# Six modulation chunks moved inside a trunk layer, and constant matrix products ahead of two waits of the router

## The chip, the cores and the metric

One core of a Trainium2 chip runs the whole program. The metric is device time in microseconds, launch to end, of that core. The program is written engine by engine: TensorE (PE in the profile), VectorE (DVE), ScalarE (ACT), GpSimd (POOL) and SyncE (SP) each have their own instruction list, and semaphores join them. All arithmetic is in float32. Weights are read from HBM while the program runs.

## What is computed

Two layers (`DEPTH = 2`) are run over 384 tokens, 128 of a context and 256 of a latent grid, with 1024 features. Cut to what the change touches:

```python
for l in range(DEPTH):
    sh1, sc1, g1, sh2, sc2, g2 = modulation(cond, P['w_mod'][l], P['b_mod'][l])
    h = rmsnorm(x, P['norm1_w'][l]) * (1 + sc1) + sh1
    u_att, u_rw, u_ssd = split_cols(h @ P['w_in'][l], [ATT_COLS, RW_COLS, SSD_COLS])
    # attention, RWKV-7 recurrence and SSD (its output goes through rmsnorm(y * silu(z)))
    x = x + g1 * (o @ P['w_out'][l])
    h = rmsnorm(x, P['norm2_w'][l]) * (1 + sc2) + sh2
    x = x + g2 * moe(h, ...)      # 16 experts, 4 groups, best group, best two experts in it
```

`modulation` is `silu(cond) @ w_mod + b_mod` with a 1024 x 6144 matrix for each layer and two rows of `cond` only: little arithmetic, but 24 MB of weights for a layer. It depends on nothing else in the layer, so it can be done anywhere before its result is read.

## The kernel before

**Layout.** Features lie on partitions and the 385 columns (`W`; one is a gap) are tokens. Weights come in items of 128 x 2048 float32 (1 MB) through homes in on-chip memory: five slots of a ring, and, in the experts' stage, three places in `sb_u`, four in `sb_arena`, one in `sb_sq` and one in `sb_hT`. From attention to the fourth column block of the output projection only ring slots 0 and 1 are open to dense items (`KEPT = 2`), since the mixers use the rest as scratch.

**Modulation chunks.** Each layer's modulation is cut into 12 chunks. A chunk (`mod` in `fill`, L1032) is two weight items and 64 recorded products `sb_ring,sb_scond` of 128 columns, whose stationary tile is 32 wide; ScalarE then copies the result to `mod_rows`. One place later a product with the identity (`modT`, L1006) turns it, and VectorE adds the bias (`sb_mod`); for chunks 3 and 9 VectorE also computes a scale (`scale1`, `scale2`). The table `MOD_AT` (L58) says how many chunks lie at each of the named places, and each engine calls `fill(l, place)` at that place in its list.

**Order of one layer on TensorE.** `mean_square` 1; `in_projection`; `attention`; `RW_ORDER` (`rw_order`, L150), a hand-written interleaving of the batched inverses, six recurrence steps (each: `values`, `carry`, `solve`, `state`, `output`; the last has no `state`) and SSD's small steps; `mixer_ends` (L1379: RWKV's group norm `gnm` and `gnv`, SSD's outputs `ys` for three tiles, then SSD's mean square `yms`); `out_projection` (eight blocks `out`); `mean_square` 2; `moe` (router logits `lg`, 24 transposes `hm`, nine small products `pos` that count tokens ahead of each token, the gather `xp` by products with a 0/1 matrix, then the experts: 12 blocks, up to 11 more for full experts, and four held ones).

**What sets the order around the change.** On VectorE, `ssd_states` (new SSD states) stands ahead of the last `carry`, whose result the last `solve` needs. SSD's gate on VectorE (`ssd_gate`) makes the squares that `yms` needs; ScalarE turns `yms` into a root (`inverse_root`: Ln, a table load, Exp), `ssd_norm` writes `sb_o` and releases `mix_ready`, on which the output projection waits. Behind `hm`, TensorE waits for `assigned_ready`, set by a chain of some 36 small VectorE instructions (`routing`); `pos` feeds a second such chain, which ends in `picks_ready`, on which the gather waits. The chunks at place `rows` stand between `pos` and the gather.

**The load order.** `weight_stream` lists the items in the order of their use, `homes_of` (L403) gives each a home by least recent use, and SP issues the loads in one list; each waits until the item that was in its home has been read (`home_free`). PSUM's eight banks are given out in the order of the same plan (`open_bank`).

Of the kernel before, what the change touches and what calls it, by code (L numbers as in the profile page):

```python
# [16 lines left out]
TILES = 3  # L17
# [36 lines left out]


MOD_CHUNKS = 12
MOD_PLACES = ["start", "norm1", "sc0", "sc2", "pv1", "pv2", "rw", "rw2", "ssd", "norm2", "rows", "held", "tail"]
MOD_AT = {(0, "start"): 2, (0, "norm1"): 2, (0, "sc0"): 1, (0, "sc2"): 1, (0, "pv1"): 1, (0, "pv2"): 1,  # L58
          (0, "rw"): 1, (0, "rw2"): 1, (0, "ssd"): 1, (0, "norm2"): 1, (0, "rows"): 2, (0, "tail"): 1,
          (1, "norm1"): 1, (1, "sc0"): 1, (1, "sc2"): 1, (1, "pv1"): 1, (1, "pv2"): 1, (1, "rw"): 1,  # L60
          (1, "ssd"): 1, (1, "norm2"): 1, (1, "rows"): 1}

# [85 lines left out]
def rw_order():  # L150

    out = []
    behind = {0: [], 2: [("factors", 0), ("factors", 1)] + recurrence(0) + recurrence(1),
              4: [("factors", 2), ("factors", 3)] + recurrence(2) + recurrence(3)}
    for first in (0, 2, 4):
        extra = behind[first]
        for n, step in enumerate(RW_STEPS):
            out += [(step, first), (step, first + 1)] + SSD_BESIDE.get((first, step), [])
            k = -(-len(extra) // (len(RW_STEPS) - n))
            out += extra[:k]  # L160
            extra = extra[k:]
    out += [("ssd_ends", 0), ("factors", 4), ("factors", 5)] + recurrence(4)
    return out + [("ssd_states", 0)] + recurrence(5)


RW_ORDER = rw_order()
# [41 lines left out]
def psum_plan():  # L208
# [4 lines left out]
    def g(consumer, *key):  # L213
        plan.append((key, consumer))
# [5 lines left out]
    for l in range(DEPTH):  # L220
# [100 lines left out]
        for t in range(1, TILES):  # L321
            for grp in range(2):
                g("v", "ys", l, t, grp)
        g("a", "yms", l)
        for n in range(KT):
            g("v", "out", l, n)
# [76 lines left out]
def homes_of(stream, plan):  # L403
# [48 lines left out]
    def free_at(n):  # L452

        if before[n] is not None:
            return order_of[stream[before[n]][1]]
        l = stream[n][0][1]
        return order_of["ms", l, 2] if HOMES[home[n]][0] == "sq" else order_of["hm", l, TILES - 1, 1]

    for l in range(DEPTH):
        first = [n for n in loads if stream[n][0][:2] == ("expert", l) and  # L460
                 (HOMES[home[n]][0] in ("sq", "hT") if before[n] is None else stream[before[n]][0][0] == "fixed")]
        at = sorted(loads.index(n) for n in first)
        assert at == list(range(at[0], at[0] + len(at)))
        loads[at[0]:at[0] + len(at)] = sorted(first, key=lambda n: (free_at(n), n))
        more = [n for n in loads if stream[n][0][:2] == ("expert", l) and stream[n][0][2] >= EXPERTS]
        loads = [n for n in loads if n not in more]
        at = loads.index(next(n for n in loads if stream[n][0] == ("expert", l, STORED, 0)))
        loads[at:at] = more
# [4 lines left out]
def program(nc, a):  # L473
# [6 lines left out]
    with ctx:  # L480
# [506 lines left out]
        def _(pe):  # L987
# [17 lines left out]
            def tr(out, in_, n=P):  # L1005
                return nc.tensor.transpose(out, in_, C("ident")[0:n, 0:n])  # L1006

            def mean_square(l, which):

                bank = open_bank(pe, "ms", l, which)  # L1010
                if which == 1 and l:
                    for t, (lo, hi) in enumerate(TILE_COLUMNS):
                        pe.wait_ge(xsq_ready, KT * 2 * l + t + 1)
                        for k in range(KT):
                            last = mm(bank[:, lo:hi], C("ones"), sq[:, k, lo:hi], k == 0, k == KT - 1)
                else:
                    for k in range(KT):
                        pe.wait_ge(xsq_ready, KT * (2 * l + which - 1) + k + 1)
                        last = mm(bank[:, 0:W], C("ones"), sq[:, k, :], k == 0, k == KT - 1)
                last.then_inc(psum_filled, 1)  # L1020
                if which == 1 and l:
                    fill(l, "start")
                fill(l, f"norm{which}")
# [355 lines left out]
            def mixer_ends(l):  # L1379
# [10 lines left out]
                fill(l, "ssd")  # L1390
                ssd_output(l, 1)
                ssd_output(l, 2)
                bank = open_bank(pe, "yms", l)
                pe.wait_ge(gated_sq_ready, l + 1)
                for i in range(2):
# [34 lines left out]
            def moe(l):  # L1430
# [17 lines left out]
                            tr(bank[:, 0:32 * TILES], logits, 32 * TILES).then_inc(psum_filled, 1)  # L1448

                bank = open_bank(pe, "pos", l)  # L1450
                pe.wait_ge(assigned_ready, l + 1)
                for t in range(TILES):
                    for i in range(t):
# [7 lines left out]
                def gathered():  # L1461

                    for k in range(KT // 2):
                        bank = open_bank(pe, "xp", l, k)
                        if k == 0:
                            pe.wait_ge(picks_ready, l + 1)
                            taken(pe, "hm", l, TILES - 1, 1)
                        for i in range(2):
# [144 lines left out]
        def _(act):  # L1613
# [295 lines left out]
            for l in range(DEPTH):  # L1909
# [10 lines left out]
                logarithms(both, 64, "eps_gn", [("gnv", l, i) for i in range(2)])  # L1920
                f(both, both, ACT.Exp, scale=-0.5).then_inc(gn_root_ready, 1)
                fill(l, "ssd")
                inverse_root(ssd_root, 256, "eps", "yms", l)
                squares(l, 2)
                moe(l)
# [3 lines left out]
        def _(dve):  # L1929
# [676 lines left out]
            for l in range(DEPTH):  # L2606
# [48 lines left out]
                ssd_output(l, 1)  # L2655
                ssd_output(l, 2)
                ssd_gate(l)
                rwkv_output(l)
                ssd_norm(l)
                for n in range(KT):  # L2660
# [174 lines left out]
```

## Time and profile before

| | |
|---|---|
| median of 3 runs | 1154.85 us (1154.1 to 1165.44) |
| the profiled execution: its time | 1162.96 us |
| its span in the trace | 1161.2 us |
| mean granted clock of TensorE, as a share of full speed | 0.932 |
| busy share of the span: PE, PE weight loads, DVE, ACT, POOL | 86%, 59%, 41%, 25%, 7% |
| data moved by DMA | 238.58 MB, 205 GB/s on average |

The profile holds one execution. Its page gives, for 40 equal slices of the span (29 us each), the busy share of each engine in tenths, the clock that TensorE was granted and the load of the 16 DMA engines. The timeline lists instructions in order of time, neighbours of one kind merged ("x16" are 16 records; a float32 product leaves two records), with the idle time of the engine ahead of them in brackets and what ended it. TensorE's records are split into products (PE) and weight loads (PEld). [...]

### The profile page before, as it was taken

Reading aid. Unit: us, or ns where it says so; the run is one execution under the profiler, and the core shown is the slowest. Engines: PE = TensorE matmul, PEld = TensorE weight load, DVE = VectorE, ACT = ScalarE, POOL = GpSimd, SP = SyncE. Lnnn points to the kernel's source line nnn. Section 1 sums busy time; section 2 is a strip of 40 time slices with the busy share of each in tenths; the row PEclk is TensorE's granted clock in tenths of the full one; section 3 lists DMA queues with packets and bytes.
Section 4 is the critical chain, followed back from the end, with each engine's and each line's share of the span. In section 5 each row is a group of like instructions: output and inputs, shape, how many; then the busy total and the mean of one; then the engine's idle time right before and its main releaser. Section 6 shows DMA issues by size and latency. Waiting matters only on the chain. (4 is left out here: it accounts for less than half of the span.)

```text
span 1161.2 us, 24556 instructions
## 1 busy us (share of the span) xinstructions
PE 1000.5 (86%) x10657; PEld 685.0 (59%) x10657; DVE 481.0 (41%) x1331; ACT 294.9 (25%) x610; POOL 78.8 (7%) x127
## 2 busy tenths in 40 slices
PE   3999999988879789867989998999987968996686
PEld 2555657788545575534755565778864556653365
DVE  1261567487431433111636166647843142311125
ACT  2331335432210511110143133543221141111000
POOL 0000000000000032221000000000000002221110
PEclk7999999999879799998999999899998978999789
DMA  9769433212156489999742221222025647999992
GB/s 385 267 157 302 108 109 146 80 72 81 60 225 263 181 323 333 361 378 376 290 176 73 73 77 73 110 111 76 8 76 238 244 173 268 385 352 375 359 410 63
DMA packets 41908, 238.58 MB, mean 205 GB/s; under 512 B 5121, under 2 KB 8193, under 8 KB 18369
## 3 DMA queue, kind: packets, MB, share of 16 engines
q1 hardware_dynamic: 29904, 196.27, 44.9%
q0 software_dynamic: 11888, 40.64, 11.3%
q8 instruction: 89, 1.46, 0.5%
q14 instruction: 27, 0.21, 0.1%
HBM read 210.15 MB, written 26.74 MB: 204 GB/s over the span
## 5 line engine op out<-in xcount | busy, mean ns | idle before, releaser
L1003 PE MATMUL bank<-sb_hT,sb_ring 128*128 128x385 f32 (+1 forms) x640 | 214.6, 493 | 4.4 <-ACT sb_hT L1623 4.4
L1003 PEld LDWEIGHTS bank<-sb_hT,sb_ring 128*128 128x128 f32 (+1 forms) x640 | 119.9, 189 | 94.0 <-issue 13.4
L1003 PE MATMUL bank<-sb_ring,sb_arena 128*64 128x256 f32 (+4 forms) x768 | 118.4, 411 | 24.8 <-DMA sb_ring<-weights 13.0
L1623 ACT ACTIVATE sb_arena<-bank 128x128 f32<-128x128 f32 (+5 forms) x108 | 44.4, 426 | 307.3 <-PE bank L1003 242.6
L1003 PEld LDWEIGHTS bank<-sb_ring,sb_arena 128*64 128x64 f32 (+2 forms) x768 | 70.6, 155 | 61.0 <-issue 31.3
L1623 ACT ACTIVATE sb_u<-bank 128x256 f32<-128x256 f32 (+3 forms) x104 | 47.7, 475 | 217.7 <-PE bank L1003 208.0
L1003 PE MATMUL bank<-sb_arena 64*64 64x64 f32 (+5 forms) x984 | 91.0, 329 | 6.1 <-DVE sb_arena L2508 1.9
L1003 PE MATMUL bank<-sb_o,sb_ring 128*128 128x385 f32 x256 | 88.6, 509 | 8.0 <-issue 8.0
L1940 DVE TENSOR_TENSOR sb_arena<-sb_arena,bank 128x128 f32<-128x128 f32 x67 | 17.8, 286 | 159.0 <-ACT sb_arena L1623 152.0
L1003 PEld LDWEIGHTS bank<-sb_o,sb_ring 128*128 128x128 f32 x256 | 50.8, 199 | 46.8 <-issue 15.0
L1943 DVE SCALAR_TENSOR_TENSOR sb_xT<-bank,sb_mod,sb_xT 128x128 f32<-128x128 f32 (+1 forms) x128 | 37.8, 360 | 92.1 <-PE bank L1003 92.0
L1003 PEld LDWEIGHTS bank<-sb_arena 64*64 64x64 f32 (+2 forms) x984 | 56.7, 146 | 31.9 <-issue 19.6
L1003 PE MATMUL bank<-sb_u,sb_arena 64*64 64x64 f32 (+2 forms) x760 | 65.1, 318 | 7.0 <-DMA sb_u<-weights 2.4
L1003 PE MATMUL bank<-sb_ring,sb_scond 128*32 128x128 f32 x1536 | 54.1, 299 | 12.5 <-DMA sb_ring<-weights 12.3
L1003 PE MATMUL bank<-sb_u 64*64 64x64 f32 x1592 | 55.7, 224 | 5.8 <-DVE sb_u L1940 4.4
L1003 PEld LDWEIGHTS bank<-sb_u 64*64 64x64 f32 x1592 | 51.3, 139 | 12.1 <-DVE sb_u L1940 6.3
L1003 PE MATMUL bank<-sb_u,sb_o 64*128 64x128 f32 (+2 forms) x576 | 51.6, 292 | 6.6 <-issue 6.1
L1003 PEld LDWEIGHTS bank<-sb_ring,sb_scond 128*32 128x32 f32 x1536 | 45.8, 120 | 19.0 <-issue 9.4
L1003 PE MATMUL bank<-sb_sq,sb_consts 128*128 128x385 f32 (+2 forms) x148 | 45.2, 456 | 11.4 <-DVE sb_sq L1940 6.0
L2624 DVE COPY sb_u<-bank 128x385 f32<-128x385 f32 x20 | 11.2, 558 | 102.1 <-PE bank L1003 102.1
L1003 PEld LDWEIGHTS bank<-sb_u,sb_o 64*128 64x128 f32 (+2 forms) x576 | 44.7, 183 | 14.0 <-issue 9.1
L1003 PEld LDWEIGHTS bank<-sb_u,sb_arena 64*64 64x64 f32 (+1 forms) x760 | 38.6, 137 | 24.2 <-issue 14.8
(209 smaller groups left out, 1238.1 us busy)
## 6 DMA issues: line engine op xcount, KB each, us to landing
sb_ring<-weights SPq DMA_DIRECT2D x116, 1024.0 KB, 8.4
sb_arena<-weights SPq DMA_DIRECT2D x29, 1024.0 KB, 18.4
sb_u<-weights SPq DMA_DIRECT2D x20, 1024.0 KB, 11.7
sb_sq<-weights SPq DMA_DIRECT2D x8, 1024.0 KB, 17.0
sb_hT<-weights SPq DMA_DIRECT2D x8, 1024.0 KB, 19.3
x_slots<-sb_o POOLq DMA_DIRECT2D x1, 6912.0 KB, 39.7
y_slots<-sb_arena POOLq DMA_DIRECT2D x54, 128.0 KB, 7.1
sb_sq<-x_slots POOLq DMA_DIRECT2D x18, 256.0 KB, 7.8
```

Of the source, the lines that this page charges most:

```text
L1003: return nc.tensor.matmul(out, lhsT, rhs, start=start, stop=stop, skip_group_check=True)
L1623: return nc.scalar.activation(out, in_, func, **kw)
L1940: return v.tensor_tensor(out, x, y, op)
L1943: return v.scalar_tensor_tensor(out, x, s, y, op0, op1)
L2624: v.tensor_copy(u[:, tile, 1:W + 1], bank[:, 0:W]).then_inc(read("u", l, c), 1)
```

## The change

The table of chunks gets two new places. `rw3` lies in the last recurrence step, behind `carry`, and `gate` lies behind SSD's last output, ahead of `yms`. Place `rows` is emptied in both layers (two chunks in layer 0, one in layer 1), and so is `norm2` in layer 1. Since chunks are dealt out in order, layer 0 now does its chunk 10 at `rw3`, its chunk 11 at `ssd`, and layer 1's chunks 0 and 1 at `gate` and `norm2`; layer 1 does its chunks 9, 10 and 11 at `rw3`, `ssd` and `gate`. The number of chunks is the same. In the planner, an expert's item may now have a ring slot as its first home (it then waits for `mix_ready`), and such items are sorted in with the others.

`keep_warm` is new: products of two constants, 128 x 128 by 385 columns, into a bank that the next real product overwrites. Five stand ahead of the wait for `assigned_ready`, seven ahead of the wait for `picks_ready`.

```diff
-MOD_PLACES = ["start", "norm1", "sc0", "sc2", "pv1", "pv2", "rw", "rw2", "ssd", "norm2", "rows", "held", "tail"]
+MOD_PLACES = ["start", "norm1", "sc0", "sc2", "pv1", "pv2", "rw", "rw2", "rw3", "ssd", "gate", "norm2", "rows", "held", "tail"]
 MOD_AT = {(0, "start"): 2, (0, "norm1"): 2, (0, "sc0"): 1, (0, "sc2"): 1, (0, "pv1"): 1, (0, "pv2"): 1,
-          (0, "rw"): 1, (0, "rw2"): 1, (0, "ssd"): 1, (0, "norm2"): 1, (0, "rows"): 2, (0, "tail"): 1,
+          (0, "rw"): 1, (0, "rw2"): 1, (0, "rw3"): 1, (0, "ssd"): 1, (0, "gate"): 1, (0, "norm2"): 1, (0, "tail"): 1,
           (1, "norm1"): 1, (1, "sc0"): 1, (1, "sc2"): 1, (1, "pv1"): 1, (1, "pv2"): 1, (1, "rw"): 1,
-          (1, "ssd"): 1, (1, "norm2"): 1, (1, "rows"): 1}
+          (1, "rw3"): 1, (1, "ssd"): 1, (1, "gate"): 1}
...
-    return out + [("ssd_states", 0)] + recurrence(5)
+    out += [("ssd_states", 0)]
+    for step in recurrence(5):
+        out.append(step)
+        if step[0] == "carry":
+            out.append(("fill", "rw3"))
+    return out
...
+        fill(l, "gate")
         g("a", "yms", l)
...
-        return order_of["ms", l, 2] if HOMES[home[n]][0] == "sq" else order_of["hm", l, TILES - 1, 1]
+        return order_of[{"ring": ("yms", l), "sq": ("ms", l, 2), "hT": ("hm", l, TILES - 1, 1)}[HOMES[home[n]][0]]]
...
-                 (HOMES[home[n]][0] in ("sq", "hT") if before[n] is None else stream[before[n]][0][0] == "fixed")]
+                 (HOMES[home[n]][0] in ("sq", "hT", "ring") if before[n] is None else stream[before[n]][0][0] == "fixed")]
...
+            def keep_warm(bank, n):
+
+                for _ in range(n):
+                    mm(bank[:, 0:W], C("head"), C("restart"))
...
                 ssd_output(l, 2)
+                fill(l, "gate")
                 bank = open_bank(pe, "yms", l)
                 pe.wait_ge(gated_sq_ready, l + 1)
...
                 bank = open_bank(pe, "pos", l)
+                keep_warm(bank, 5)
                 pe.wait_ge(assigned_ready, l + 1)
...
                         if k == 0:
+                            keep_warm(bank, 7)
                             pe.wait_ge(picks_ready, l + 1)
...
                 fill(l, "ssd")
+                fill(l, "gate")
                 inverse_root(ssd_root, 256, "eps", "yms", l)
...
                 ssd_gate(l)
+                fill(l, "gate")
                 rwkv_output(l)
```

The last two hunks are in ScalarE's list and in VectorE's, the three before them in TensorE's.

## Rows read from the trace of the kernel before

**Rows 1.** The page's 40 slices: granted TensorE clock, DMA load.

```profile
PEclk7999999999879799998999999899998978999789
DMA  9769433212156489999742221222025647999992
```

**Rows 2.** Windows of the experts' stages: stretch, length, busy of engines, clock, DMA share, GB/s.

```profile
410.00:430.00 20.00, 17.25 (x151) 14.39 (x141) 5.05 (x18) 4.48 (x11) 6.60 (x6) 1.00 0.96 370
...
510.00:530.00 20.00, 13.07 (x87) 6.84 (x87) 2.23 (x6) 2.45 (x5) 4.16 (x8) 0.83 1.02 363
...
1060.00:1080.00 20.00, 9.32 (x72) 4.96 (x68) 2.09 (x5) 1.99 (x5) 4.04 (x8) 0.80 1.02 347
```

**Rows 3.** Timeline, last recurrence step, both layers: start, length, instruction, idle before.

```profile
299.20 0.40 PE L1003 MATMUL bank<-sb_arena,sb_hT 64*64 64x64 f32 x12
...
301.90 0.68 PE L1003 MATMUL bank<-sb_tmp,sb_u 64*64 64x64 f32 x16 [2.29 <-DVE sb_tmp L1940]
...
853.36 1.07 PE L1003 MATMUL bank<-sb_tmp,sb_u 64*64 64x64 f32 x16 [2.29 <-DVE sb_tmp L1940]
```

**Rows 4.** Timeline, group norm (gnm) and the chunk at ssd, both layers.

```profile
305.32 2.90 PE L1003 MATMUL bank<-sb_arena,sb_consts 128*128 128x385 f32 x4 [0.80 <-DVE sb_arena L2327]
...
311.49 0.14 PEld L1006 LDWEIGHTS bank<-sb_consts,sb_mod_rows 128*128 128x128 f32 x1
...
312.01 1.95 PE L1003 MATMUL bank<-sb_ring,sb_scond 128*32 128x128 f32 x64
...
857.79 1.53 PE L1003 MATMUL bank<-sb_arena,sb_consts 128*128 128x385 f32 x4 [0.81 <-DVE sb_arena L2327]
...
862.52 1.95 PE L1003 MATMUL bank<-sb_ring,sb_scond 128*32 128x128 f32 x64
```

**Rows 5.** Timeline, SSD's mean square (yms) and what follows; its twin in layer 1.

```profile
325.88 2.90 PE L1003 MATMUL bank<-sb_sq,sb_consts 128*128 128x385 f32 x4 [2.65 <-DVE sb_sq L1940]
...
331.27 1.41 DVE L1943 SCALAR_TENSOR_TENSOR sb_o<-sb_arena,sb_small 128x128 f32<-128x128 f32 x4 [1.70 <-ACT sb_arena L1623]
...
332.78 12.56 PE L1003 MATMUL bank<-sb_o,sb_ring 128*128 128x385 f32 x30 [4.00 <-issue]
...
876.40 1.98 PE L1003 MATMUL bank<-sb_sq,sb_consts 128*128 128x385 f32 x4 [2.65 <-DVE sb_sq L1940]
```

**Rows 6.** Timeline, norm2 of layer 1, router and gather, and two full-clock references.

```profile
934.62 0.17 DVE L1943 SCALAR_TENSOR_TENSOR sb_scale<-sb_mod,sb_consts 128x16 f32<-128x16 f32 x1
...
401.73 3.99 PE L1003 MATMUL bank<-sb_arena,sb_consts 128*128 128x16 f32 x18 [4.85 <-DVE sb_arena L1940]
...
405.75 0.21 DVE L2457 COPY sb_arena<-bank 128x48 f32<-128x48 f32 x1 [4.18 <-PE bank L1003]
...
413.67 10.60 PE L1003 MATMUL bank<-sb_u,sb_o 128*128 128x256 f32 x48 [1.95 <-issue]
...
963.63 13.50 PE L1003 MATMUL bank<-sb_u,sb_o 128*128 128x256 f32 x48 [4.18 <-issue]
...
926.52 5.35 PE L1003 MATMUL bank<-sb_sq,sb_consts 128*128 128x385 f32 x16
...
85.06 0.82 PE L1006 MATMUL bank<-sb_consts,sb_arena 128*128 128x128 f32 x6
```

**Rows 7.** Windows of layer 0 between two changes of the clock, columns as in Rows 2.

```profile
303.90:310.60 6.70, 5.90 (x35) 3.73 (x32) 3.69 (x10) 0.40 (x1) 0.00 (x0) 0.50 0.00 0
...
392.70:396.00 3.30, 3.30 (x17) 3.30 (x16) 0.66 (x5) 2.84 (x5) 0.00 (x0) 0.50 0.23 97
396.10:399.40 3.30, 0.78 (x7) 0.54 (x5) 2.82 (x17) 1.59 (x4) 0.00 (x0) 1.00 0.44 117
...
401.80:405.70 3.90, 3.90 (x19) 3.90 (x19) 0.00 (x0) 0.00 (x0) 0.00 (x0) 0.50 0.00 0
```

**Rows 8.** DMA issues: KB each, median us to landing; at 313.9 us, and the page's.

```profile
sb_ring<-weights SPq DMA_DIRECT2D x1, 1024.0 KB, 4.8
...
sb_u<-weights SPq DMA_DIRECT2D x20, 1024.0 KB, 11.7
```

## The prediction

> **What bounds the kernel now.** I read the page's 40 slices first, for what kind of time each stage is made of [rows 1]. The clock row tells that TensorE is not held at full speed everywhere: slices of 7 and 8 tenths stand in the middle of both layers, around the end of the recurrence and the router. The DMA row tells the stages apart: it stands at 9 in the experts' stages and at 1 or 2 in the mixers. Then windows of the experts' stages [rows 2]: the transfers are saturated there (0.96 to 1.02), and TensorE is busy for 17.25 of 20 us at their start, but only for 13.07 and 9.32 us later. So this stage is bound by the transfers, and what precedes it by TensorE and by chains through VectorE and ScalarE. The change touches only the second kind. I therefore went to the timeline and looked, at each of the four places, for the idle time of TensorE and for the clock that it has behind it [rows 3 to 7].
>
> **Can the experts' stage swallow what is saved ahead of it?** Its transfers go on from slot to slot: a home is loaded again when its item has been read. Nine homes outside the ring and five in it are full of early experts' items before the first expert is computed, in both versions, and the first reload waits for the first expert's products. So stage and transfers start together, and a start that is t earlier ends t earlier. I let every saving pass.
>
> **The last recurrence step (rw3).** TensorE ends `carry` at 299.20 + 0.40 = 299.60 us and starts `solve` at 301.90, 2.29 us later, since VectorE does SSD's states first; layer 1 is alike [rows 3]. A turn and a chunk take 312.01 + 1.95 - 311.49 = 2.47 us at full clock [rows 4], the chunk alone 1.95. In layer 0 both go in (chunk 9 still has to be turned): 0.17 us late. In layer 1 there is no turn: 0. VectorE's bias (0.17 us, with chunk 9 also a scale of 0.17) and ScalarE's copy fall where both wait for `solve`. If the items were late or the clock low, the cover would be gone: the chunk would cost up to its own 1.95 us. The gain is the clock behind it. In layer 0 the idle stretch is followed by one at 0.50, from 303.9 to 310.6, and the group norm's products take 2.90 us [rows 4, 7]; in layer 1 they take 1.53. From gnm to the chunk at ssd it is 312.01 - 305.32 = 6.69 us in layer 0, less 311.49's turn ahead of the chunk (0.52), and 862.52 - 857.79 = 4.73 us in layer 1: 1.44 us to gain. Layer 1 pays earlier: from `solve` to gnm it takes 857.79 - 853.36 = 4.43 us against 305.32 - 301.90 = 3.42: 1.01 us to gain. But chunk 9's turn now stands ahead of layer 1's chunk at ssd, where TensorE has no gap: -0.5 (the 0.52 of layer 0). Sum: layer 0 +1.27, layer 1 +0.5.
>
> **Ahead of yms (gate).** TensorE idles 2.65 us in both layers [rows 5]; turn and chunk take 2.47: no cost. yms itself takes 2.90 us in layer 0 and 1.98 in layer 1; at full clock 1.53, as its twin gnm of the same shape [rows 4, 5]: 1.38 and 0.45 us. Behind yms stand Ln, a table load, Exp and VectorE's last step at 331.27, for which VectorE had waited 1.70 us. With the new bias ahead of it (0.17) it has 1.53 us left, so the 1.38 passes. Queued behind the two turns and copies is nothing else that is late. The chunk costs something elsewhere: it fills both open slots, so the first two items of the output projection can only be asked for when it has been read, at about 325.7 instead of 314.0. One item of 1 MB, asked for with idle queues, lands in 4.8 us [rows 8]: 330.5. It is wanted at 332.78 - 1.38 + 0.1 = 331.4 or so: 0.9 us to spare. The output projection's own cold start stays: the 4.00 us gap ahead of it is as long as before [rows 5].
>
> **norm2 of layer 1.** Without its chunk, the scale of chunk 9 (934.62, 0.17 us) leaves the head of VectorE's list [rows 6]: +0.2 us. The logits are paced by ScalarE, so the longer idle stretch of TensorE ahead of them costs nothing.
>
> **Five constant products and pos.** The idle time ahead of pos is 4.85 us, and pos takes 3.99 us for 18 records, at a clock of 0.50 [rows 6, 7]. A product of 385 columns takes 5.35 / 8 = 0.67 us at full clock [rows 6] and 2.90 / 2 = 1.45 at half [rows 5]. Five take 3.3 us: hidden. The clock at the end of the transposes is 1.00, and it fell during the idle stretch [rows 7]; if the five hold it, pos takes something between half of 3.99, 2.0, and 18 times 0.82 / 6, 2.5 us [rows 6]. I take 2.2: +1.8 us in each layer, all of it on the path, since VectorE waits 4.18 us for pos. Bounds: no gain if the clock falls again before pos, and 2.0.
>
> **Seven constant products, and the gather without chunks.** From pos to the gather it is VectorE's chain, 413.67 - 405.75 = 7.9 us. The chunks taken out were hidden by it (1.95 us of idle time behind them in layer 0, 4.18 in layer 1), so their removal alone gives nothing. Seven products take 4.7 us: hidden, with 2.8 us of idle time in layer 0 (behind one turn) and 3.2 in layer 1. The gather took 10.60 us with a gap of 1.95 ahead of it, and 13.50 with one of 4.18 [rows 6]. New gaps lie between: a gap of 2.65 us lost the clock ahead of yms in layer 0 (2.90 us) and half kept it in layer 1 (1.98) [rows 5]. I take the mean, 12.05, for each layer: -1.45 and +1.45, together 0; bounds 2 x 10.60 and 2 x 13.50, that is +2.9 and -2.9.
>
> [...] In the last slice before the idle stretch TensorE did nothing but transposes, at 0.50, and behind it the clock was 1.00 [rows 7]. [...]
>
> **The sum.** Layer 0: 1.27 + 1.38 + 1.8 - 1.45 = 3.0. Layer 1: 0.5 + 0.45 + 0.2 + 1.8 + 1.45 = 4.4. Together 7.4 us. The profiled execution took 1162.96 us, so it would take 1155.6; it is 8.1 us above the median of the runs, for reasons that one trace can't show. Taken off the median, 1154.85, the sum gives 1147.5 us.
>
> **Rivals.**
> - *The constants run at half clock.* Five then take 7.25 us against the 4.85 of the gap: pos starts 2.4 us late and gains at most 2.0. The 1.8 us turn into -0.6 in both layers, 4.8 us less: 1152.3. For it: pos itself, busy throughout, did not raise the clock (401.8 to 405.7 at 0.50 [rows 7]), and seven products at half clock take 10.2 us, more than the chain's 7.9. Against it: the 1.00 at 396.1. [...]
> - *The clock also holds to the gather.* Both gathers take 10.6 us, 2.9 more: 1144.6.
> - *The change doesn't do what it says.* The clock falls in the same places, only elsewhere in each: covers cost their 0.17 + 0.5 and give 0.2, so 1155.3. For it: group norm in layer 1 stood at full clock though it had no chunk [rows 4], so idle time alone doesn't decide.
> - *The head start of the transfers.* Four items in layer 0 and two in layer 1 are no longer loaded at the router. At 370 GB/s [rows 2] an item of 1.05 MB is 2.8 us: if the experts' stage were bound by its own total, layer 0 would gain up to 11 us, 1136.5. Against it: the homes are full anyway.
> - *Slower: the output projection waits for its first item.* Behind gate's chunk it lands in 4.8 us only if the queues are idle. The items of `sb_u`, asked for in bursts, landed in 11.7 [rows 8]: it would be 11.7 - 4.8 - 0.9 = 6.0 us late in each layer, 12 us: 1159.5. From a landing of 4.8 + 0.9 + 3.7 = 9.4 us on this mechanism alone makes the kernel slower. Against it: no transfer but these runs there.
>
> **Chances.** Forecast 0.47; clock holds to the gather 0.17; constants at half clock 0.13; no effect 0.10; head start 0.06; first item late 0.07. The range 1141 to 1156 us takes in the bounds of the gathers (2.9 us) and of pos, and the second, third and fourth case; it leaves out the head start and most of the late item. About one per cent (11.5 us) is what a measurement of this kernel can tell from no change. Faster by more needs the head start or the upper bounds together: 0.2. Slower by more needs a late item with an even longer landing, or a stall that I don't see: 0.05. The rest, 0.75, is within 1%.
>
> **What would show each step.** In the profile after: chunks in the two gaps, with `solve` less than 0.3 us later behind `carry`; gnm at about 1.5 us and a clock of 1.00 behind it in both layers; yms at 1.5 us; the first block of the output projection not waiting for a DMA; pos at 2.0 to 2.5 us; seven products that end ahead of the gather; the gathers between 10.6 and 13.5 us. The forecast is wrong if pos stays at 4 us, if the wait ahead of the output projection grows beyond 4 us, or if the experts' stage, from the first expert to the layer's end, changes its length by more than 2 us: then the saving was eaten or multiplied there.

## The result, and the profile after

The changed kernel took 1142.74 us (median of 4 runs, 1138.7 to 1143.35), the kernel before 1154.47 us in 4 runs beside it. The ratio of changed to before is 0.9863, with a 95% interval of 0.9818 to 0.9908: faster by 1.4%. Ratios, here and below, are taken over the fast runs alone, those at most 1.5% above the fastest run of their kernel on that chip, and so are not the quotients of the medians given beside them (1142.74 / 1154.47 is 0.990). The forecast was 1147.5 us, 0.6% faster. The time lies inside the range, but the gain is 1.4% by the ratio, which is 16 us, and 11.7 us by these medians, where 7.4 were forecast, and "faster by over 1%" had been given 0.2. Counted chunk by chunk, seven have a new place, four of those done in layer 0 and three of those done in layer 1, not the six of the title.

The profiled execution took 1142.84 us (span 1141.0), 20 us less than that of before. The page's clock and DMA rows, to be read against [rows 1]:

```profile
PEclk9999998999999889998999999999999979999889
DMA  9769532422169449999842221232027736999992
```

Of the five 7s of the clock row one is left, far into layer 1. (The first of the five stood at the very start, where nothing was changed.) The DMA row looks much as before; what it hides comes below.

The timeline of TensorE in the profile after, at the places of the change: the last recurrence step and the group norm in layer 0, then in layer 1 (to be read against [rows 3, 4]):

```profile
305.60 0.40 PE L1009 MATMUL bank<-sb_arena,sb_hT 64*64 64x64 f32 x12
305.94 0.33 PE L1012 MATMUL bank<-sb_consts,sb_mod_rows 128*128 128x128 f32 x1
306.19 1.96 PE L1009 MATMUL bank<-sb_ring,sb_scond 128*32 128x128 f32 x64
308.30 0.69 PE L1009 MATMUL bank<-sb_tmp,sb_u 64*64 64x64 f32 x16
...
311.70 1.53 PE L1009 MATMUL bank<-sb_arena,sb_consts 128*128 128x385 f32 x4 [1.00 <-DVE sb_arena L2342]
...
842.65 0.68 PE L1009 MATMUL bank<-sb_tmp,sb_u 64*64 64x64 f32 x16 [0.41 <-ACT sb_mod_rows L1637]
...
845.99 1.53 PE L1009 MATMUL bank<-sb_arena,sb_consts 128*128 128x385 f32 x4 [0.93 <-DVE sb_arena L2342]
```

Turn and chunk fill the gap. In layer 0 `solve` follows the chunk without a gap, in layer 1, where no turn stands, 0.41 us behind it. Next, the chunk at gate, yms and the output projection in both layers (against [rows 5]), and constants, pos and gather (against [rows 6]):

```profile
327.96 1.95 PE L1009 MATMUL bank<-sb_ring,sb_scond 128*32 128x128 f32 x64
330.43 1.53 PE L1009 MATMUL bank<-sb_sq,sb_consts 128*128 128x385 f32 x4 [0.51 <-DVE sb_mod L1955]
335.95 1.62 PE L1009 MATMUL bank<-sb_o,sb_ring 128*128 128x385 f32 x2 [4.00 <-DVE sb_o L1958]
...
864.71 1.53 PE L1009 MATMUL bank<-sb_sq,sb_consts 128*128 128x385 f32 x4 [0.51 <-DVE sb_mod L1955]
870.25 5.17 PE L1009 MATMUL bank<-sb_o,sb_ring 128*128 128x385 f32 x10 [4.00 <-DVE sb_o L1958]
...
398.39 3.40 PE L1009 MATMUL bank<-sb_consts 128*128 128x385 f32 x10
403.84 3.87 PE L1009 MATMUL bank<-sb_arena,sb_consts 128*128 128x16 f32 x18 [2.05 <-DVE sb_arena L1955]
407.80 6.22 PE L1009 MATMUL bank<-sb_consts 128*128 128x385 f32 x14
415.62 10.63 PE L1009 MATMUL bank<-sb_u,sb_o 128*128 128x256 f32 x48 [1.60 <-DVE sb_u L1955]
...
938.22 2.49 PE L1009 MATMUL bank<-sb_arena,sb_consts 128*128 128x16 f32 x18 [1.31 <-DVE sb_arena L1955]
940.55 6.15 PE L1009 MATMUL bank<-sb_consts 128*128 128x385 f32 x14
948.65 10.63 PE L1009 MATMUL bank<-sb_u,sb_o 128*128 128x256 f32 x48 [1.95 <-DVE sb_u L1955]
```

The output projection waits for `sb_o` and for no transfer, 4.00 us as before. pos is 3.87 us in layer 0 and 2.49 in layer 1. Both gathers take 10.63 us.

Where do the 20 us between the two profiled executions lie? The table gives stretches from the start of one step on TensorE to the start of the next (in the last row to the end of the last product), in us, out of the timelines of five kernels: before, the changed one in two executions, and two of the experiments below.

| layer, stretch | before | changed | changed again | chunks only | constants only |
|---|---|---|---|---|---|
| 0, start to gnm | 305.32 | 311.70 | 309.11 | 306.41 | 308.12 |
| 0, gnm to yms | 20.56 | 18.73 | 18.72 | 18.73 | 18.72 |
| 0, yms to output projection | 6.90 | 5.52 | 5.52 | 5.52 | 5.65 |
| 0, output projection to pos | 68.95 | 67.89 | 67.95 | 69.10 | 69.17 |
| 0, pos to gather | 11.94 | 11.78 | 11.65 | 11.94 | 13.85 |
| 0, gather to the tail's chunk | 162.96 | 155.87 | 155.07 | 156.32 | 159.02 |
| 1, tail's chunk to gnm | 281.16 | 274.50 | 275.26 | 279.96 | 273.54 |
| 1, gnm to yms | 18.61 | 18.72 | 18.72 | 18.72 | 20.59 |
| 1, yms to output projection | 5.98 | 5.54 | 5.53 | 5.53 | 6.91 |
| 1, output projection to pos | 69.26 | 67.97 | 68.81 | 68.00 | 69.32 |
| 1, pos to gather | 11.99 | 10.43 | 10.92 | 11.97 | 12.00 |
| 1, gather to the last product | 189.36 | 185.00 | 182.96 | 187.40 | 186.10 |

Two things stand out that the forecast did not have: layer 0's stretch behind the gather is 7 us shorter, and the two long stretches in which next to nothing was changed (start to gnm, tail's chunk to gnm) differ by 6 to 8 us between executions, in either direction.

### The profile page after: what moved, and what is told of

Same layout as the page of the kernel before. It is cut to its first block and busy times, and to the rows that moved or that the text cites. A ratio compares the mean times of both kernels' runs of the same rounds, so it can differ in the third digit from the quotient of the medians.

```text
span 1141.0 us, 24651 instructions
## 1 busy us (share of the span) xinstructions
PE 999.4 (88%) x10705; PEld 682.7 (60%) x10705; DVE 480.8 (42%) x1331; ACT 295.7 (26%) x610; POOL 79.1 (7%) x127
## 3 DMA queue, kind: packets, MB, share of 16 engines
q0 software_dynamic: 11888, 40.64, 11.7%
## 5 line engine op out<-in xcount | busy, mean ns | idle before, releaser
L1009 PE MATMUL bank<-sb_ring,sb_arena 128*64 128x256 f32 (+4 forms) x768 | 113.8, 398 | 34.4 <-PEq L1590 12.4
L1009 PE MATMUL bank<-sb_arena 64*64 64x64 f32 (+5 forms) x984 | 88.5, 323 | 5.0 <-DVE sb_arena L2523 1.9
L1009 PE MATMUL bank<-sb_ring,sb_scond 128*32 128x128 f32 x1536 | 50.9, 286 | 12.5 <-DMA sb_ring<-weights 12.4
L1009 PEld LDWEIGHTS bank<-sb_ring,sb_scond 128*32 128x32 f32 x1536 | 42.9, 115 | 18.0 <-issue 8.4
L1009 PE MATMUL bank<-sb_u,sb_o 64*128 64x128 f32 (+2 forms) x576 | 49.1, 287 | 4.6 <-DVE sb_u L1955 3.6
```

Source lines behind the costliest of these rows:

```text
L1009: return nc.tensor.matmul(out, lhsT, rhs, start=start, stop=stop, skip_group_check=True)
```

## Experiments

Each kernel ran beside the kernel before on the same chip, in five rounds. The kernel before had medians, over all its runs, of 1162.57 us (29 runs, 1148.57 to 1167.76), 1157.06 (16 runs) and 1162.52 (11 runs) on the three chips: the first for sections 1 and 2, the second for the changed kernel again, the loads held in layer 0, more constants and the tail's chunk at norm2, the third for the rest.

### 1. The chunks alone, and the constants alone

The change without its constants:

```diff
-                keep_warm(bank, 5)
-                            keep_warm(bank, 7)
```

> The changed kernel without its twelve constant products in a layer: only the chunks stand at their new places. Three theories of the 11.7 us that the change brought (1154.5 to 1142.7). (Sum as forecast) The chunks bring 1.27 + 1.38 us in layer 0 and 0.5 + 0.45 + 0.2 in layer 1, 3.8 together: about 1150.7; layer 0 from the gather to the tail's chunk as long as before, 163 us. (Head start of the transfers) Emptying the place rows frees the queues at the start of the experts' stage: layer 0 from gather to tail is about 156 us as after the change, 7 us shorter, and the kernel takes 1144 to 1147 us. (Constants carry it) The clock that the constants hold is worth more than forecast, and the chunks alone bring nothing or less, since the gathers then start cold: 1152 us or more.

Measured: 1150.24 us, ratio 0.9895 (0.9848 to 0.9942). The time alone would fit "Sum as forecast", but that was counted from a kernel before of 1154.5 us, and here it took 1162.57: the gain is 12 us, not 4, and the stretch behind the gather is the 156 us of the head start. Next, the kernel before with these two lines added, and nothing else:

> The kernel before with the five and seven constant products in each layer and every chunk at its old place, the rows' chunks between pos and the seven. (Sum as forecast) pos gains up to 1.8 us in a layer and the gather of layer 1 up to 2.9: 3.6 to 6.5 us, 1148 to 1151 us; in layer 0 two chunks, a turn and seven constants (about 4 + 0.5 + 4.7 = 9.2 us) exceed the 7.9 us of VectorE's chain, which costs 1.3 there. (Head start) The constants bring at most 2 or 3 us; the experts' stage of layer 0 stays at 163 us from gather to tail: about 1152. (Constants carry it) 8 us or more: 1146 or less.

Measured: 1154.19 us, ratio 0.9942 (0.9909 to 0.9974). On one chip the chunks are thus worth about 12 us (1.05% of 1160), the constants 7 (0.58%): both work, and together they are 1.6%, where the whole change had measured 1.4%. The table has the places: with the chunks alone layer 0 is 156.3 us from the gather to the tail's chunk, as with the whole change. With the constants alone it is 159.0, but the gather starts 1.9 us late there (two chunks and seven products exceed VectorE's chain: 13.85 against 11.94). No theory had the 159.0: from pos to the tail's chunk it is 172.9 us with the constants alone, 174.9 before and 168.3 with the chunks alone, and of the 2.0 us to before pos itself has 1.4 (2.63 for 3.99). "Constants carry it" has fallen; the head start is supported, not yet shown.

### 2. The place rows filled again, or emptied alone

No constants; chunks at rw3, ssd and gate in layer 0, and two at rows again:

```diff
+          (0, "rw"): 1, (0, "rw2"): 1, (0, "rw3"): 1, (0, "ssd"): 1, (0, "gate"): 1, (0, "norm2"): 1,
+          (0, "rows"): 2, (0, "tail"): 1,
+          (1, "sc0"): 1, (1, "sc2"): 1, (1, "pv1"): 1, (1, "pv2"): 1, (1, "rw"): 1,
+          (1, "rw3"): 1, (1, "ssd"): 1}
```

> No constants; chunks at rw3, ssd and gate of layer 0 as in the change, but two chunks stand again at rows of layer 0, with their four loads; layer 1 gives up the two at norm1 and gate for it, so the work is the same in total. To be read against the run without constants whose rows are empty. (Head start) layer 0 from gather to tail is 5 to 7 us longer than in that run, with a DMA share of 1.0 and not 0.8 in the first 20 us behind the gather; the kernel is 4 to 7 us slower than that run, less what two chunks fewer in layer 1 give. (Sum as forecast) the chunks at rows lie under VectorE's chain: layer 0 from gather to tail is the same within 1 us in both.

Measured: 1160.72 us, ratio 0.9994 (0.9957 to 1.0032), against 0.9895 for the chunks alone. Gather to tail: 162.91 us, 6.6 more than there, with a DMA share of 0.99 in the first 20 us behind the gather and not 0.75. The whole kernel is 10.5 us slower, more than the 4 to 7 expected: the chunks alone took 279.96 us from the tail's chunk to gnm of layer 1 and this run 284.63, and here the chunk at sc0, now the first of layer 1, waits 2.67 us for a weight item. So the stretch, and not the total, tells what rows is worth. Then the kernel before with rows emptied into the tail:

```diff
-          (0, "rw"): 1, (0, "rw2"): 1, (0, "ssd"): 1, (0, "norm2"): 1, (0, "rows"): 2, (0, "tail"): 1,
+          (0, "rw"): 1, (0, "rw2"): 1, (0, "ssd"): 1, (0, "norm2"): 1, (0, "rows"): 0, (0, "tail"): 3,
```

> The kernel before with one edit: the two chunks at rows of layer 0 are done at its tail, where one chunk stands already; no new places, no constants. (Head start) From gather to the tail's first chunk layer 0 takes 156 to 158 us and not 163; two more chunks at the tail cost 2 x 1.95 us of TensorE and up to 2 x 5.6 us of loads, so the kernel as a whole stays within 4 us of the one before. (Sum as forecast) 163 us as before, and the kernel 0 to 4 us slower.

Measured: 1162.43 us, ratio 1.002 (0.9983 to 1.0057). Gather to tail is 156.48 us, 6.5 less than before; but from the first chunk of the tail to layer 1's first query norm it takes 623.50 - 570.20 = 53.30 us, where before took 622.34 - 576.63 = 45.71. The 6.5 us are given back 50 us later. So it matters whether a load leaves the whole stretch of saturated transfers, which reaches from the gather to layer 1's projection; moved inside it, it gave nothing.

### 3. Loads held back, nothing else changed

Rows' chunks are products, waits and loads at once. This run parts them: in the changed kernel, four expert items of layer 0 are asked for only when pos is there.

```diff
+def held_back(where):
+    return where in (("expert", 0, 2, 2), ("expert", 0, 4, 0), ("expert", 0, 4, 1), ("expert", 0, 3, 2))
...
+        if held_back(stream[n][0]):
+            return order_of["pos", 0]
...
+                if held_back(stream[n][0]):
+                    filled(sp, "pos", l)
```

> The changed kernel as it is, once more, as the reference of the three runs beside it. The last four profiles put layer 0 from the gather to the tail's chunk at 156.3 and 156.5 us where no chunk stands at rows, and at 159.0 and 162.9 where two do. (Head start) that stretch is again 156 us. What varies from one execution to the next is told by two stretches that the change does not touch: from the chunk at sc0 to the turn at sc2 (20.9 us with the clock up, 3 to 5 us more where it fell in the idle stretch of 2.67 us) in either layer. Time: 1139 to 1146 us.

> The changed kernel with one edit: the four expert items of layer 0 that it loads into ring slots right behind the output projection and behind norm2's chunk wait until pos has been counted, about where the kernel before could first ask for theirs. No product, no wait of TensorE and no chunk differ. (Head start, by when these loads can start) layer 0 from the gather to the tail's chunk goes from 156 to 161 to 163 us and the kernel is 5 to 7 us slower than the changed one. (Head start, by the number of bytes: four items fewer in the stretch, not when they are loaded) also slower, since these four now lie in the stretch: this run doesn't tell the two apart. (Sum as forecast: the homes are full anyway, or the chunks' products at rows were the cost) 156 us and no difference.

Measured: the changed kernel again 1138.2 us, ratio 0.9853 (0.9806 to 0.99), its six runs between 1134.45 and 1139.57; with the loads held 1146.99, ratio 0.9908 (0.9869 to 0.9948): 8.8 us slower. The gather and the tail's chunk in the changed kernel, then with the loads held:

```profile
412.95 10.63 PE L1009 MATMUL bank<-sb_u,sb_o 128*128 128x256 f32 x48 [1.48 <-DVE sb_u L1955]
...
568.02 1.95 PE L1009 MATMUL bank<-sb_ring,sb_scond 128*32 128x128 f32 x64
```

```profile
413.58 10.63 PE L1017 MATMUL bank<-sb_u,sb_o 128*128 128x256 f32 x48 [0.60 <-DVE sb_u L1963]
...
575.86 1.95 PE L1017 MATMUL bank<-sb_ring,sb_scond 128*32 128x128 f32 x64
```

155.07 us against 162.28: the time at which four loads start is worth 7.2 us, with TensorE's own work unchanged. The windows show how: 25 us from 10 us ahead of the gather, then the 15 us behind (length, busy of the engines, clock, DMA share, GB/s). The changed kernel again, then the loads held, then before:

```profile
402.90:427.90 25.00, 22.73 (x108) 17.40 (x109) 8.39 (x37) 3.93 (x9) 8.78 (x10) 0.89 0.46 158
427.90:442.90 15.00, 13.55 (x106) 8.74 (x104) 3.96 (x11) 0.83 (x3) 2.09 (x4) 1.00 1.01 381
```

```profile
403.50:428.50 25.00, 23.60 (x109) 17.76 (x111) 8.38 (x37) 3.92 (x9) 6.81 (x7) 0.86 0.77 294
428.50:443.50 15.00, 13.55 (x106) 8.78 (x104) 3.92 (x11) 0.83 (x3) 4.03 (x8) 1.00 0.95 272
```

```profile
403.70:428.70 25.00, 22.25 (x222) 19.16 (x223) 8.45 (x38) 4.48 (x11) 6.60 (x6) 0.88 0.72 283
428.70:443.70 15.00, 13.55 (x108) 8.71 (x105) 4.07 (x11) 0.83 (x3) 4.24 (x8) 1.00 0.97 309
```

Four items are 4.2 MB. In the first 25 us the run with held loads moves 136 GB/s x 25 us = 3.4 MB more, in the next 15 us 109 x 15 = 1.6 MB less. It is 4.2 - 3.4 + 1.6 = 2.4 MB behind, and at some 360 GB/s [rows 2] that is 6.7 of the 7.2 us, as an estimate. The smaller part is that the transfers stand idle ahead of the gather in the changed kernel, its homes being full (a DMA share of 0.00 from 402.90 to 412.95 us), and the held loads don't quite fit into that gap. The larger one is a lower rate, 272 for 381 GB/s, at nearly the same share of busy time. What else is in the queues then? The DMA issues of those 15 us (KB each, median us to landing), in the changed kernel again and with the loads held:

```profile
sb_arena<-weights SPq DMA_DIRECT2D x4, 1024.0 KB, 10.4
sb_u<-weights SPq DMA_DIRECT2D x3, 1024.0 KB, 6.4
sb_sq<-weights SPq DMA_DIRECT2D x1, 1024.0 KB, 14.2
y_slots<-sb_arena POOLq DMA_DIRECT2D x4, 128.0 KB, 6.4
```

```profile
sb_arena<-weights SPq DMA_DIRECT2D x4, 1024.0 KB, 17.9
sb_u<-weights SPq DMA_DIRECT2D x3, 1024.0 KB, 13.5
sb_sq<-weights SPq DMA_DIRECT2D x1, 1024.0 KB, 22.0
sb_sq<-x_slots POOLq DMA_DIRECT2D x2, 256.0 KB, 8.8
sb_hT<-x_slots POOLq DMA_DIRECT2D x2, 256.0 KB, 11.5
y_slots<-sb_arena POOLq DMA_DIRECT2D x4, 128.0 KB, 7.5
```

The four writes to `y_slots` stand in both. But four reads of tokens (`x_slots`) now fall among the first reloads of weights; before has the same four there. In the changed kernel they are through by then: asked for in the 25 us before those 15, they land in 4.3 and 5.0 us, where the run with held loads has 8.8 and 11.5. Every weight item lands 7 to 8 us later after its issue: a backlog of 7 us, which the stage carries to its end. That the token reads are what lowers the rate is the reading that fits; no run moved them alone.

The same in layer 1, for the two items that before loads behind rows' chunk there:

> The changed kernel with one edit in layer 1 alone: the two expert items that the kernel before could only load behind the chunk at rows wait until pos is there. (Head start, in proportion) four items held gave 7.2 us in layer 0, so two give 3 to 4 us here: gather to the last product 186.5 us where the changed kernel took 183 and 185, ratio to before 0.989. (Layer 1's stage has slack) its stage ends on a chain through the slots (a wait of 8 to 9 us for x_slots in both kernels) and not on the bytes: 183 to 185 us, ratio 0.985.

Measured: 1139.69 us, ratio 0.9805 (0.9763 to 0.9847); gather to the last product 182.01 us, where the changed kernel took 185.00 and 182.96. Nothing is lost: layer 1's stage has slack, and what it gained, 189.36 to 185, is mostly its gather (13.50 to 10.63).

### 4. What the five products are worth

The changed kernel without the five ahead of pos:

> The changed kernel without the five constant products ahead of pos; the seven ahead of the gather stay. (Seven carry the constants' gain) the seven end warm anyway: both gathers 10.6 us; pos goes from 2.5 to 3.9 us back to 3.99 in both layers. Layer 0 loses little (pos took 3.7 to 3.9 there with the five too), layer 1 about 1.3 us: ratio to before 0.986 to 0.988, where the changed kernel had 0.985 and 0.986. (The five hold the clock for what follows) the seven, started at half clock behind pos, don't bring it up in time: a gather of 12 us or more in one layer and a ratio of 0.989 or more.

Measured: 1142.51 us, ratio 0.9825 (0.9779 to 0.9871), beside 1139.69 for the kernel with two loads held. pos is 3.99 us again (at 402.75, behind 4.76 idle), and the seven take 6.74 us, since they start at half clock (0.50 from 406.8 to 410.0 us), but both gathers take 10.63. So the seven warm the gather alone; pos to gather is 11.89 and 11.94 us, so the five are worth 0.1 to 0.3 us in layer 0 and 1.0 to 1.5 in layer 1.

### 5. The idle stretches that were left, and a faster kernel

The clock also falls where the change has put nothing. In attention TensorE waits 2.67 us for the first probabilities. The value products behind it in before, layer 0 and layer 1:

```profile
172.07 2.14 PE L1003 MATMUL bank<-sb_ring,sb_arena 128*128 128x128 f32 x16 [2.67 <-DVE sb_ring L1940]
...
721.02 3.76 PE L1003 MATMUL bank<-sb_ring,sb_arena 128*128 128x128 f32 x16 [2.67 <-DVE sb_ring L1940]
```

The gap is the same. In layer 0 the granted clock was 1.00 through the gap and the products, in layer 1 it was 0.87 over the gap and 0.50 over the products, and from the chunk at sc0 to that at sc2 it took 26.31 us for 20.88, 5.4 us longer. In the 11 profiles of kernels that leave this gap open (2.67 or 2.68 us each time) these products took 2.14 us in 10 of 22 layers and 2.61 to 3.76 in 12. So this gap alone gives up to 5.4 us a layer of what varies from execution to execution. More constants, at three further places:

```diff
+                if (l, which) == (0, 1):
+                    keep_warm(bank, 3)
...
+                            if (t, g, b) == (0, 0, 0):
+                                keep_warm(bank, 3)
...
+                bank = open_bank(pe, "out", l, 0)
+                keep_warm(bank, 5)
...
-                keep_warm(bank, 5)
+                keep_warm(bank, 7)
```

The hunks are, in order, ahead of the first mean square of layer 0, ahead of attention's first value products in both layers, ahead of the output projection's wait for `mix_ready`, and ahead of pos.

> The changed kernel with constant products at three more places and two more ahead of pos: 3 ahead of the first mean square of layer 0 (gap 5.4 us, mean square 7.9 us where a warm one takes 5.35), 3 ahead of attention's first value products (gap 2.67 us, three products 2.0), 5 ahead of the output projection (gap 4.0, five 3.35), 7 and not 5 ahead of pos. (Clock) mean square -2.5 us; the stretch from the chunk at sc0 to the turn at sc2 20.9 us in both layers and in all executions, which is 0 to 8 us for one of them and 3 on average; the output projection up to 1 us in each layer; pos 2.5 us in layer 0 too, -1.4, of which the expert stage passes on what it can. Together 4 to 8 us faster than the changed kernel, and the times lie closer together. (Constants only move the fall) the clock falls elsewhere, and less than 2 us is gained.

Measured: 1130.95 us, ratio 0.9801 (0.9754 to 0.9847), 7.2 us less than the changed kernel beside it. Value products, output projection and pos of layer 0:

```profile
168.45 2.21 PE L1009 MATMUL bank<-sb_consts 128*128 128x385 f32 x6
171.10 2.23 PE L1009 MATMUL bank<-sb_ring,sb_arena 128*128 128x128 f32 x16 [0.45 <-DVE sb_ring L1962]
...
324.80 3.40 PE L1009 MATMUL bank<-sb_consts 128*128 128x385 f32 x10
328.92 7.40 PE L1009 MATMUL bank<-sb_o,sb_ring 128*128 128x385 f32 x22 [0.71 <-DVE sb_o L1965]
...
395.22 2.18 PE L1009 MATMUL bank<-sb_arena,sb_consts 128*128 128x16 f32 x18 [1.27 <-DVE sb_arena L1962]
```

From the chunk at sc0 to that at sc2 it takes 20.88 us in both layers. pos takes 2.18 us in both, and the output projection to norm2's mean square 41.59 where the changed kernel took 43.2 to 44.1: 1.6 to 2.5 us in a layer, against the 1 that I had expected. One place got worse: with pos warm, layer 1's seven end sooner, leave 3.32 us idle, and the gather takes 12.31 us and not 10.63. The first mean square did not follow (7.00 us), and the times lie no closer together: six runs within 6.5 us, those of the changed kernel beside it within 5.1. Five products instead of three there:

> As the run with more constants (1130.95 us, ratio to before 0.980), but five and not three constant products ahead of the first mean square of layer 0. With three they took 3.14 us, left 2.6 us idle, and the mean square took 7.0 us. Five end less than 1 us ahead of it. (Clock) it takes 5.35 us: 1.6 us faster, ratio 0.979, layer 0's start to gnm 303 us. (No effect) 7.0 us again.

Measured: 1131.14 us, ratio 0.9736 (0.9696 to 0.9775); the mean square takes 7.14 us, since the five, at a granted clock of 1.00, take hardly longer than the three had (3.40 and 3.14 us, where three ahead of the value products took 2.21) and leave 2.62 us idle, where less than 1 had been expected. Over that idle stretch the granted clock was still 1.00; it was 0.50 from 27.5 to 29.0 us, within the mean square. No effect.

> The changed kernel with layer 0's tail chunk done at norm2, beside the one that stands there, so that the expert stage and the turn to layer 1 load two items (2 MB) less. (Bytes in the saturated stretch) where the tail got two chunks more, layer 1's first mean square came 7.6 us later; one less gives up to 3.8 us: 2 to 4 us faster than the changed kernel, if norm2's second chunk (1.95 us, its items with room in five slots) hides under ScalarE's work. (The gain was only from freeing the slots ahead of the gather) now two more chunk items stand ahead of the experts' first loads in the queue and the kernel is 0 to 3 us slower.

```diff
-          (0, "rw"): 1, (0, "rw2"): 1, (0, "rw3"): 1, (0, "ssd"): 1, (0, "gate"): 1, (0, "norm2"): 1, (0, "tail"): 1,
+          (0, "rw"): 1, (0, "rw2"): 1, (0, "rw3"): 1, (0, "ssd"): 1, (0, "gate"): 1, (0, "norm2"): 2, (0, "tail"): 0,
```

Measured: 1140.32 us, ratio 0.9882 (0.9826 to 0.9938), 2.1 us more than the changed kernel, with six runs from 1132.99 to 1144.72: no gain, and a loss that the runs don't tell from none. Gather to layer 1's first query norm is 198.3 us against 199.3 in the changed kernel beside it and 201.6 in its other profile, so the saturated stretch got shorter by 1.0 to 3.3 us; norm2 to pos got longer by 1.5. Last, the chunk goes where there is idle time ahead of the router, into attention's gap:

```diff
-MOD_AT = {(0, "start"): 2, (0, "norm1"): 2, (0, "sc0"): 1, (0, "sc2"): 1, (0, "pv1"): 1, (0, "pv2"): 1,
-          (0, "rw"): 1, (0, "rw2"): 1, (0, "rw3"): 1, (0, "ssd"): 1, (0, "gate"): 1, (0, "norm2"): 1, (0, "tail"): 1,
-          (1, "norm1"): 1, (1, "sc0"): 1, (1, "sc2"): 1, (1, "pv1"): 1, (1, "pv2"): 1, (1, "rw"): 1,
+MOD_AT = {(0, "start"): 2, (0, "norm1"): 2, (0, "sc0"): 1, (0, "sc1"): 1, (0, "sc2"): 1, (0, "pv1"): 1, (0, "pv2"): 1,
+          (0, "rw"): 1, (0, "rw2"): 1, (0, "rw3"): 1, (0, "ssd"): 1, (0, "gate"): 1, (0, "norm2"): 1,
+          (1, "norm1"): 1, (1, "sc0"): 1, (1, "sc1"): 1, (1, "sc2"): 1, (1, "pv2"): 1, (1, "rw"): 1,
```

> As the run beside it with five constants first, but the gap of 2.67 us ahead of attention's first value products holds a chunk instead of three constants (new place sc1, behind the second scores). Layer 0's chunk comes from its tail, layer 1's from pv1. (Bytes in the saturated stretch) layer 0 from the gather to the first of the query norms of layer 1, 199 to 202 us with the tail's chunk, gets shorter by up to 3.6 us, since two items are no longer moved in it; layer 1's stretch from sc2's turn to pv1's (12.08 us with a chunk) loses up to 1.95. Together 2 to 5 us faster than the run beside it. (Slots) a ring slot is loaded again in 4.8 us and only two slots are open: the chunk at sc1 waits for its items, and with it the value products: 0 to 6 us slower.

Measured: 1124.53 us (1121.84 to 1128.44), ratio 0.9678 (0.9638 to 0.9718): 6.6 us less than the run beside it, and the fastest kernel here, by more than the 2 to 5 expected. In the profiles 1.5 us of it lie between the gather and layer 1's first query norm (200.62 for 202.14, although the gather itself, behind 3.22 us idle, took 12.31 us for 10.63), and 3.6 from there to gnm (225.11 for 228.66). No slot was late; layer 0:

```profile
169.05 0.33 PE L1011 MATMUL bank<-sb_consts,sb_mod_rows 128*128 128x128 f32 x1
169.31 2.26 PE L1008 MATMUL bank<-sb_ring,sb_scond 128*32 128x128 f32 x64
171.87 2.14 PE L1008 MATMUL bank<-sb_ring,sb_arena 128*128 128x128 f32 x16 [0.30 <-DVE sb_ring L1957]
```

## Why the prediction was right or wrong

**The experts' stage swallows nothing and gives nothing: wrong, and this is the step that failed.** "Nine homes outside the ring and five in it are full of early experts' items before the first expert is computed, in both versions" was not so. With chunks at rows, four ring slots of layer 0 can be loaded again only once those chunks are read, at 409 to 412 us, and those loads stand in the queues beside the tokens'; without, all are there and the transfers rest (158 GB/s for 25 us around the gather in the changed kernel, against 283 in the kernel before). The price is 7.1 us in the two profiles, 7.2 with the loads held. I had the case as the rival with the head start, at 0.06, and set it aside by that sentence alone. It would have been checked by following each slot in the load order: which item it holds when the gather starts. The rival's 11 us, four times 2.8, was too much: 3.4 of the 4.2 MB still fit into the 25 us around the gather. The test that I had named for it, a stage that changes by more than 2 us, is the one that showed it. In layer 1 the step holds: two loads held there cost nothing.

**The last recurrence step: right.** The cover held as worked out (`solve` starts 0.41 us behind the chunk or at once, and no later behind `carry` than before), gnm takes 1.53 us in both layers. But layer 0's 1.44 us were not a fixed sum. With no chunk at rw3, gnm to yms took 20.56, 18.61, 18.72, 20.59, 20.10 and 18.61 us in the two layers of before, of the constants alone and of rows moved to the tail: the clock fell in three of six (gnm in 2.90 or 2.91 us and not 1.53). With one it takes 18.72 or 18.73, each time. That is 0.8 us in a layer on average. The stretch ahead, from `solve` to gnm, has to be added: it took 3.33 to 4.48 us in the same six layers, 3.8 on average, and 3.3 to 3.4 with the chunk. Together that is 1.3 us in a layer on average, which is layer 0's forecast and more than the 0.5 of layer 1; between the two profiles it is 1.85 and 1.0.

**Ahead of yms: right.** 1.53 us in both layers, all of it passed on: yms to the output projection 5.52 us for 6.90 and 5.98. No item was late. Not forecast: the output projection to pos is 1.0 us shorter in about half the layers of the changed kernels, since the clock sometimes comes back sooner behind the 4.00 us (at 1.00 from the fifth or sixth microsecond of the output projection on in the profile after, from the seventh in the one before).

**norm2 of layer 1: right.** From its mean square to pos it is 24.72 us for 25.12, 0.4 where 0.2 had been forecast.

**pos: wrong in layer 0, right in layer 1.** The five ran at full clock (3.40 us) and were hidden, and the granted clock was still 1.00 in the 2.05 us of idle time behind them. It fell with pos itself, to 0.71 over its first 0.46 us and 0.50 from there: 3.87 us for the 2.2 forecast. In layer 1 the rest was 1.31 us and pos took 2.49. Not 1.8 us twice, but 0.2 and 1.6 (from pos to the gather, 11.78 for 11.94 and 10.43 for 11.99). The lower bound had it.

**The gather: the step is right, the value too low.** 10.63 us in both layers, by gaps of 1.60 and 1.95 us: the rival "the clock also holds to the gather" with its 2.9 us. That the seven started at half clock (0.50 from 407.8 to 409.5 us), and took 6.2 us and not 4.7, cost nothing. These two misses nearly cancel: from the output projection's start to the end of both gathers the two profiles differ by 1.2 + 5.7 = 6.9 us, of which 4.6 are pos, its chain and the gathers, where 3.6 had been forecast.

**The rival that the constants run at half clock: it did not come, for the five.** They ran at full clock, and it had risen while TensorE did transposes: in layer 0 the granted clock was 0.50 from 392 to 395 us, where the transposes begin (at 394.16), 0.67 from 395.0 to 398.3, where they alone run, and 1.00 behind. The five took 3.40 us in both layers, where the rival had 7.25.

**The base of the sum.** I took the 7.4 us off the median of three runs, 1154.85, and called the profiled execution's 1162.96 high. Later medians of the same kernel, on three chips, are 1162.57, 1157.06 and 1162.52: it was the three runs that were low. The changed kernel has 1142.74 and 1138.2, and the two ratios, 0.9863 and 0.9853, make the gain 16 to 17 us. By the stretches of the profiles that is, as an estimate, some 4 from the chunks' clock, some 5 to 6 from the constants, 7 from the loads. The forecast has the first two with 7.4 us, a little low, and lacks the third.

## What to carry to other kernels

Where a stage is bound by transfers, ask what each buffer holds when the stage begins, slot by slot: filler work that is free on its engine may hold the slots in which the next stage's loads should already lie. A load moved within the saturated stretch gave nothing here; one moved out of it gave at most the time of its bytes, less what fitted into idle time anyway (7.2 us for four items, 1.0 to 3.3 for two, where 2.8 us each is the time of the bytes). Filler with loads of its own belongs into the idle time of the mixers, and products of constants where no chunk fits; what counted here was the idle time that was left behind them, not their number: ahead of the first mean square three left 2.60 us idle and five 2.62, and it took 7.00 and 7.14 us (more in the next section).

## What the hardware showed that I had not expected

The same idle stretch of 2.67 us ended with the clock held in 10 of 22 cases (value products in 2.14 us) and fallen in 12 (2.61 to 3.76 us), and one of 3.2 to 3.3 us cost the gather 1.7 us each of three times (12.31 us for 10.63), where up to 1.96 us cost it nothing. pos, 18 records of 16 columns, was more delicate. In the 18 layers with constants ahead of it, it took 2.18 us behind 0.5 to 1.3 us idle, 2.5 to 3.1 behind 1.3 to 1.7, and 3.7 to 4.0 behind 2.0 to 2.3. In the changed kernel's layer 0 the clock outlasted the idle time (1.00 over its 2.05 us) and fell in pos (0.50 from 0.46 us on), although TensorE was busy in it throughout. That filled gaps bring the runs closer together is not shown: six runs of the kernels with more constants lie within 4.9 to 6.6 us, but so do those of the changed kernel (5.1); the kernel before has 19 to 29 us between its extremes, in 11 to 29 runs. And the DMA engines' busy share was no measure of their work: at 0.95 to 1.01 they moved 272 GB/s in one execution and 381 in another, in the same 15 us of the same kernel but for the start of four loads.
